# Later GpSimd clearings, a prepared double norm, a shorter output norm in the delta rule, and dilated attention's copies, scores and maxima re-ordered

## The reference

```python
# between the blocks: the last norm of the first, then the first norm of the second
x = rmsnorm(x, g_final)
h = rmsnorm_2(x, norm_mix[0])

# the end of the delta rule: 8 heads of 128, forward and backward sums
o = jnp.transpose(o_fwd + o_bwd, (0, 2, 1, 3))
o = o * lax.rsqrt(jnp.mean(o * o, axis=-1, keepdims=True) + RMS_EPS)
o = o * norm_w.astype(f32) * jax.nn.silu(z.astype(f32))
return o.reshape(B, S, H * DV).astype(h.dtype) @ w_out

# dilated attention: 3 groups of heads (dilation 1, 4, 16), 6 heads each
s = jnp.einsum('nbqhe,nbkhe->nbhqk', qb, kw).astype(jnp.float32) * (E ** -0.5)
s = s + bias[None, None]
m = jnp.max(s, axis=-1, keepdims=True)
lse = m + jnp.log(jnp.sum(jnp.exp(s - m), axis=-1, keepdims=True))
p = jnp.exp(s - lse)
o = jnp.einsum('nbhqk,nbkhe->nbqhe', p.astype(v.dtype), vw)
alpha = jax.nn.softmax(jnp.stack(lses, axis=2), axis=2)
```

## Time and profile before

| what | value |
|---|---|
| median of 3 runs | 1920.75 us (1918.34 to 1920.76) |
| the profiled execution | 1922.57 us, span from first to last instruction 1920.8 us |
| TensorE busy | 1862.0 us, 97% of the span |
| VectorE, ACT, GpSimd busy | 1312.5 us (68%), 907.3 us (47%), 22.6 us (1%) |
| mean granted TensorE clock | 0.984 of full |
| HBM | 161 GB/s over the span |

### The profile page before, as it was taken

The page is one execution under the profiler, slowest core; times in us unless marked ns, Lnnn a source line. Parts: engine busy times, 40 slices in busy tenths (PEclk is TensorE's granted clock), DMA queues, the critical chain, the costliest instruction groups (busy, mean ns, idle before and its releaser), DMA issues. The chain is left out here.

```text
span 1920.8 us, 30237 instructions
## 1 busy us (share of the span) xinstructions
PE 1862.0 (97%) x12455; PEld 1699.2 (88%) x12455; DVE 1312.5 (68%) x2105; ACT 907.3 (47%) x1233; POOL 22.6 (1%) x25
## 2 busy tenths in 40 slices
PE   7999999999999999999999989999899999999998
PEld 7999898999999999988888879878888889779887
DVE  5657874999788888755555567986577455647754
ACT  6457633342444343444444455766365343445533
POOL 0000000000000000000000000010000001000000
PEclk9999999999999999999999998997999999999999
DMA  6444344444444444465555552420254456615543
GB/s 231 176 157 157 132 176 177 153 179 173 154 154 141 148 153 154 154 229 197 191 188 191 194 202 91 152 88 24 73 190 175 177 214 201 146 69 205 187 164 152
DMA packets 44755, 310.63 MB, mean 162 GB/s; under 512 B 5182, under 2 KB 5694, under 8 KB 8160
## 3 DMA queue, kind: packets, MB, share of 16 engines
q1 hardware_dynamic: 42592, 303.58, 43.2%
q0 software_dynamic: 1472, 4.86, 1.6%
q10 hardware_dynamic: 576, 0.55, 0.1%
HBM read 306.84 MB, written 2.13 MB: 161 GB/s over the span
## 5 line engine op out<-in xcount | busy, mean ns | idle before, releaser
L310 DVE TENSOR_TENSOR s_ring_lo<-s_ring,s_w_hi 128x2048 fp32r<-128x2048 f32 x233 | 533.4, 2290 | 190.7 <-ACT s_w_hi L304 186.2
L304 ACT ACTIVATE s_w_hi<-s_ring 128x2048 fp32r<-128x2048 f32 x232 | 442.8, 1909 | 141.4 <-PE bank L347 46.2
L347 PE MATMUL bank<-s_h_r,s_w_hi 128*128 128x256 f32 x2944 | 391.0, 286 | 0.3 <-DVE s_arena L3454 0.3
L347 PEld LDWEIGHTS bank<-s_h_r,s_w_hi 128*128 128x128 f32 x2944 | 368.1, 193 | 4.8 <-issue 3.6
L1711 PE MATMUL bank<-s_w_hi,s_h_r 128*128 128x512 f32 x1008 | 238.8, 389 | 0.3 <-issue 0.3
L1711 PEld LDWEIGHTS bank<-s_w_hi,s_h_r 128*128 128x128 f32 x1008 | 189.2, 188 | 39.6 <-issue 0.4
L347 PE MATMUL bank<-s_h_r,s_ring_lo 128*128 128x256 f32 x1472 | 207.0, 283 | 0.0
L347 PEld LDWEIGHTS bank<-s_h_r,s_ring_lo 128*128 128x128 f32 x1472 | 190.4, 193 | 0.0
L1813 ACT ACTIVATE s_h_r<-s_arena 128x512 fp32r (+1 forms) x64 | 40.4, 632 | 184.5 <-PE bank L1711 184.5
L2969 DVE TENSOR_TENSOR s_ring_lo<-s_ring,s_spare_r 128x2048 fp32r<-128x2048 f32 x32 | 73.1, 2291 | 77.0 <-ACT s_spare_r L2955 77.0
L1711 PE MATMUL bank<-s_ring_lo,s_h_r 128*128 128x512 f32 x504 | 124.5, 389 | 0.0
(11 more groups left out here) (448 smaller groups left out, 2446.0 us busy)
## 6 DMA issues: line engine op xcount, KB each, us to landing
s_ring<-weights SPq DMA_DIRECT2D x282, 1024.0 KB, 4.8
s_arena<-bias_by_distance POOLq DMA_DIRECT2D x12, 384.0 KB, 7.3
s_arena<-mem SPq DMA_DIRECT2D x1, 1024.0 KB, 5.7
s_x<-x SPq DMA_DIRECT2D x1, 1024.0 KB, 13.4
x_away<-s_x SPq DMA_DIRECT2D x1, 1024.0 KB, 6.4
s_arena<-sub_keys SPq DMA_DIRECT2D x1, 1024.0 KB, 8.4
s_arena<-x_away SPq DMA_DIRECT2D x1, 1024.0 KB, 6.9
out<-s_x SPq DMA_DIRECT2D x2, 512.0 KB, 2.6
```

The costliest lines, as they stand in the source:

```text
L304: act.activation(k.w_hi[:, u % 2, :], k.ring[:, u % RING, :], ACT.Copy).then_inc(k.hi_ready, 1)
L310: dve.tensor_tensor(k.ring_lo[:, u % RING, :], k.ring[:, u % RING, :], plain(k.w_hi[:, u % 2, :]), ALU.subtract).then_inc(k.lo_ready, 1)
L347: last = pe.matmul(out[:, nb * S:(nb + 1) * S], w[:, c, nb * P:(nb + 1) * P], h[:, c, :], start=(n == 0 and c == 0), stop=(n == 2 and c == 7))
```

## The change

1. The second and third clearing of GpSimd wait for the first unit of the delta rule's projection.
2. The double norm's second factor is written as 1 / (mean of the weighed squares + EPS times (mean + EPS)), which is the same number; its parts are prepared before the last squares are there.
3. In the read-out TensorE adds the state's part itself, as a product with the identity that opens the bank. ACT squares straight out of the bank and takes the root of mean + EPS in one step; VectorE takes the reciprocal and scales the outputs out of the bank; the turn is a plain transpose.
4. In the dilated layer the third group of `turn(0)` goes behind unit 11 (and its copy on ACT behind the evacuation of unit 11), `highest(4)` ahead of `weights(3)` and `split_out(1)`, and the third group of `score(5)` behind the first two of `turn(4)`.

```diff
@@ DoubleSeam.factors
-        m, t, both = self.mean[:, 0:2], self.inner[:, 0:2], self.both
+        raw, m, e, both = self.inner[:, 0:2], self.mean[:, 0:2], self.product[:, 0:2], self.both
         dve.wait_ge(self.x_squared, 4)
-        own.up(dve.tensor_tensor(m, self.x_sums[:, 0:2], self.x_sums[:, 2:4], ALU.add))
+        own.up(dve.tensor_tensor(raw, self.x_sums[:, 0:2], self.x_sums[:, 2:4], ALU.add))
         own.settle(dve)
-        own.up(dve.tensor_scalar(m, m, 1.0 / D, EPS, ALU.mult, ALU.add))
+        own.up(dve.tensor_scalar(e, raw, EPS / D, EPS * EPS, ALU.mult, ALU.add))
+        own.up(dve.tensor_scalar(m, raw, 1.0 / D, EPS, ALU.mult, ALU.add))
         own.settle(dve)
+        dve.wait_ge(self.w_squared, 2)
+        own.up(dve.scalar_tensor_tensor(out=e, in0=self.w_sums[:, 0:2], scalar=1.0 / D, in1=e, op0=ALU.mult,
+                                        op1=ALU.add))
         own.up(dve.reciprocal(both[:, 0:2], m))
+        own.settle(dve)
         dve.wait_ge(self.w_squared, 4)
-        own.up(dve.tensor_tensor(t, self.w_sums[:, 0:2], self.w_sums[:, 2:4], ALU.add))
+        own.up(dve.scalar_tensor_tensor(out=e, in0=self.w_sums[:, 2:4], scalar=1.0 / D, in1=e, op0=ALU.mult,
+                                        op1=ALU.add))
         own.settle(dve)
-        own.up(dve.tensor_tensor(t, t, both[:, 0:2], ALU.mult))
-        own.settle(dve)
-        own.up(dve.tensor_scalar(t, t, 1.0 / D, EPS, ALU.mult, ALU.add))
-        own.settle(dve)
-        own.up(dve.reciprocal(self.product[:, 0:2], t))
-        own.settle(dve)
-        dve.tensor_tensor(both[:, 2:4], self.product[:, 0:2], both[:, 0:2], ALU.mult).then_inc(self.factor_ready, 1)
+        dve.reciprocal(both[:, 2:4], e).then_inc(self.factor_ready, 1)
@@ gdn_project, gpsimd
         pool.memset(plain(g.unset), 0.0).then_inc(zeros_set, 1)
+        pool.wait_ge(k.unit_done, U["gdn_qkv"] + 1)
         pool.memset(plain(inv_r), 0.0).then_inc(inv_clear, 1)
@@ gdn_solve, tensor: read_out(q)
             pe.wait_ge(qs_out, q + 1)
+            pe.matmul(ps[4 + q][:, :], k.ident, group(from_state, q), start=True, stop=False)
...
@@ turn(q)
-            pe.wait_ge(diag_ready, q + 1)
+            pe.wait_ge(o_scaled, q + 1)
             for c in range(4):
-                last = pe.matmul(ps[q][:, c * P:(c + 1) * P], o[:, 4 * q + c, :], diag[:, q % 2, c, :],
-                                 start=True, stop=True)
+                last = pe.transpose(ps[q][:, c * P:(c + 1) * P], o[:, 4 * q + c, :], k.ident)
@@ scalar
         for q in range(GROUPS):
-            act.wait_ge(o_out, q + 1)
+            act.wait_ge(o_mm, q + 1)
             for c in range(4):
-                act.activation(junk[:, c, :], o[:, 4 * q + c, :], ACT.Square,
+                act.activation(junk[:, c, :], ps[4 + q][:, c * P:(c + 1) * P], ACT.Square,
...
-            act.wait_ge(o_means, q + 1)
-            act.activation(o_root[:, 4 * q:4 * q + 4], o_inv[:, 4 * q:4 * q + 4], ACT.Sqrt).then_inc(o_roots, 1)
+            act.wait_ge(o_square, 4 * (q + 1))
+            act.activation(o_root[:, 4 * q:4 * q + 4], o_sum[:, 4 * q:4 * q + 4], ACT.Sqrt, scale=1.0 / P,
+                           bias=o_eps[:, 0:1]).then_inc(o_roots, 1)
@@ vector
+        dve.memset(o_eps[:, 0:1], EPS).then_inc(eps_set, 1)
...
-            dve.wait_ge(o_mm, q + 1)
-            dve.wait_ge(qs_out, q + 1)
-            dve.tensor_tensor(group(o, q), ps[4 + q][:, :], group(from_state, q), ALU.add).then_inc(o_out, 1)
-            dve.wait_ge(o_square, 4 * (q + 1))
-            own.up(dve.tensor_scalar(o_mean[:, at], o_sum[:, at], 1.0 / P, EPS, ALU.mult, ALU.add))
+            dve.wait_ge(o_roots, q + 1)
+            own.up(dve.reciprocal(o_inv[:, at], o_root[:, at]))
             own.settle(dve)
-            dve.reciprocal(o_inv[:, at], o_mean[:, at]).then_inc(o_means, 1)
+            for c in range(4):
+                last = dve.tensor_scalar(o[:, 4 * q + c, :], ps[4 + q][:, c * P:(c + 1) * P],
+                                         o_inv[:, 4 * q + c:4 * q + c + 1], None, ALU.mult)
...
+            last.then_inc(o_scaled, 1)
             if q >= 1:
                 gate(q - 1)
             if q >= 2:
                 split_out(q - 2)
...
@@ ds_layer, tensor
-        turn(0)
+        turn(0, (0, 1))
         unit(11)
+        turn(0, (2,))
         score(2)
...
-        score(5)
+        score(5, (0, 1))
         turn(4, (0, 1))
+        score(5, (2,))
         weigh(3)
@@ scalar
-        turned_out(0)
+        turned_out(0, (0, 1))
         evacuate(11)
+        turned_out(0, (2,))
         turned_out(1, (0, 1))
@@ vector
         split_lo(k, dve, O)
+        highest(4)
         weights(3)
         split_out(1)
-        highest(4)
         split_lo(k, dve, O + 1)
```

More of the change, by code:

```diff
@@ L2396, in gdn_solve @@
     lay = Layout(k, g.at_kdec + 2 * H * S)
-    o, junk, diag = lay.take(2 * H, P), lay.take(4, P), lay.take(2, 4, P)
+    o, junk = lay.take(2 * H, P), lay.take(4, P)
     gated, from_state = carve(k, g.at_kdec, H, S), carve(k, g.at_kdec, 2 * H, P)
     oT = [k.spare_r[:, n * H * S:(n + 1) * H * S].rearrange("p (h s) -> p h s", h=H) for n in range(2)]
-    o_sum, o_mean, o_inv, o_root = (k.small[:, n * 16:(n + 1) * 16] for n in range(4))
+    o_sum, o_eps, o_inv, o_root = (k.small[:, n * 16:(n + 1) * 16] for n in range(4))
     names = ("decay_mm", "decays_ready", "keys_mm", "system_built", "third_turned", "solved_set",
@@ L2408, in gdn_solve @@
      wide_mm, wide_out, last_mm, level_done, v1_mm, v1_out, state_mm, state_out, ks_mm, rhs_ready, v2_mm, v2_out,
-     o_mm, o_out, o_square, o_means, o_roots, diag_ready, o_turned, o_gated, o_round, o_split,
+     o_mm, eps_set, o_square, o_roots, o_scaled, o_turned, o_gated, o_round, o_split,
      qs_mm, qs_out) = (ctx_sem(k, "g_" + n) for n in names)
@@ L2603, in read_out @@
                     pe.matmul(ps[4 + q][:, at], g.intraT[:, h, first_s[f], :], v1[:, 2 * h + f, :],
-                              start=True, stop=False)
+                              start=False, stop=False)
                     last = pe.matmul(ps[4 + q][:, at], g.intraT[:, h, second_s[s], :], v2[:, 2 * h + s, :],
-                                     start=False, stop=True)
+                                     start=False, stop=(hh == 1 and tt == TT - 1))
             last.then_inc(o_mm, 1)
         def turn(q):
-            pe.wait_ge(diag_ready, q + 1)
+            pe.wait_ge(o_scaled, q + 1)
             for c in range(4):
-                last = pe.matmul(ps[q][:, c * P:(c + 1) * P], o[:, 4 * q + c, :], diag[:, q % 2, c, :],
-                                 start=True, stop=True)
+                last = pe.transpose(ps[q][:, c * P:(c + 1) * P], o[:, 4 * q + c, :], k.ident)
             last.then_inc(o_turned, 1)
@@ L2633, in tensor @@
                 turn(q - 1)
-        pe.wait_ge(o_out, 2)
         pe.wait_ge(o_round, 2)
@@ L2638, in tensor @@
         turn(3)
-        pe.wait_ge(o_out, 4)
         pe.wait_ge(o_round, 4)
@@ L2750, in scalar @@
             act.activation(group(state, q), ps[4 + q][:, :], ACT.Copy).then_inc(state_out, 1)
+        act.wait_ge(eps_set, 1)
         act.activation(o_root[:, 0:1], k.ident[:, 0:1], ACT.Sqrt)
@@ L2886, in vector @@
             at = slice(4 * q, 4 * q + 4)
-            dve.wait_ge(o_mm, q + 1)
-            dve.wait_ge(qs_out, q + 1)
-            dve.tensor_tensor(group(o, q), ps[4 + q][:, :], group(from_state, q), ALU.add).then_inc(o_out, 1)
-            dve.wait_ge(o_square, 4 * (q + 1))
-            own.up(dve.tensor_scalar(o_mean[:, at], o_sum[:, at], 1.0 / P, EPS, ALU.mult, ALU.add))
-            own.settle(dve)
-            dve.reciprocal(o_inv[:, at], o_mean[:, at]).then_inc(o_means, 1)
+            dve.wait_ge(o_roots, q + 1)
+            own.up(dve.reciprocal(o_inv[:, at], o_root[:, at]))
+            own.settle(dve)
+            for c in range(4):
+                last = dve.tensor_scalar(o[:, 4 * q + c, :], ps[4 + q][:, c * P:(c + 1) * P],
+                                         o_inv[:, 4 * q + c:4 * q + c + 1], None, ALU.mult)
+                if c < 3:
+                    own.up(last)
+            last.then_inc(o_scaled, 1)
             if q >= 1:
@@ L2897, in vector @@
                 split_out(q - 2)
-            dve.wait_ge(o_out, q + 1)
-            dve.wait_ge(o_roots, q + 1)
-            for c in range(4):
-                last = dve.tensor_scalar(diag[:, q % 2, c, :], k.ident, o_root[:, 4 * q + c:4 * q + c + 1], None,
-                                         ALU.mult)
-                if c < 3:
-                    own.up(last)
-            last.then_inc(diag_ready, 1)
         gate(GROUPS - 1)
@@ L3191, in unit, with score @@
                 unit_N_split(k, pe, F + n, (k.hT_hi, k.hT_lo), [bank[:, 0:S], bank[:, S:2 * S]])
-        def score(j):
+        def score(j, groups=range(G)):
             rows = out_rows(j)
-            for g in range(G):
+            for g in groups:
                 q = G * j + g
```

2 lines of the change are left out of this document (1 added, 1 removed).

## The result

The changed kernel takes **1903.4 us** (median of 5 runs, 1903.26 to 1905.88), the kernel before, beside it, 1918.68 us (1913.79 to 1920.76, 5 runs): ratio 0.9917, 95% interval 0.9905 to 0.993. The forecast was 1908.0 with a range from 1904.5 to 1912.5. The profiled execution took 1904.64 us around a span of 1902.0, so the two profiled executions lie 17.9 us apart and the two medians 15.3.

What follows compares the result with a forecast made beforehand. TensorE is busy nearly throughout, so only waits in front of it count. 1.9 + 2.1 + (2.3 + 2.0 + 0.8) + 4.6 = 13.7 us off 1922.57 gives 1908.9, lowered to 1908 for the profiled run's excess; range 1904.5 to 1912.5.

Steps and rivals of the forecast that it cites:

- 1.3 + 0.6: Double norm: root starts earlier, some 1.3 us from the moved clearing and 0.6 from the shorter chain, 1.9 together.
- The hold: Projection's third unit: VectorE's tensor_scalar held by the moved clearings ends 1.2 us late; 1.4 us of cover remain, cost 0.
- The bound of 1.6 us for held splits: Projection: if VectorE's tensor_tensor splits beside the clearings were held too, the sum would lose at most 1.6 us.
- a forecast of 2.1: Delta rule's read-out: the output product's second half starts 2.1 us earlier through the shorter output norm.
- The loop: Read-out, per group: squares, root, reciprocal, scalings, gate, rounding and hand-overs through ACT and VectorE take 4.15 us.
- the identity product took over 1 us: Read-out: sign that the forecast is wrong; TensorE's 128x512 f32 product with the identity was counted at 0.88 us.
- (a): Dilated layer: with unit 11 put between, TensorE's 2.35 us wait for ACT's copies at the third turn goes; gain 2.3.
- (b): Dilated layer: with highest(4) moved ahead, TensorE's 2.00 us wait for VectorE before the third score goes; gain 2.0.
- (c): Dilated layer: score(5)'s third group behind turn(4) leaves waits of 0.4 and 0.65 in place of 1.82 us; gain 0.8.
- The rival that the clock falls all the same: Dilated layer: low clock returns despite the new order; one stretch costs 1.7 to 2.9, both 4.6: 1910 to 1912.5 us; 24%.
- term (d): Dilated layer: two stretches at 1.2 GHz go with the waits of 2.00 and 1.82 us; gain 4.6 (2.9 + 1.7).
- a low stretch elsewhere: Double norm or read-out: a shorter stretch at low clock, as their waits shrink, could take the time down to 1904.5 us.

Runs made afterwards that it cites:

- delayed by 6 steps: Changed kernel with six extra small VectorE steps ahead of the double norm's factors: 1910.16 us, ratio 0.9941.
- the spread kernels: Gates' 2 x 24 products issued in four runs of 12: on the changed kernel 1906.02 us, with six extra VectorE steps 1905.66, with the read-out's gate first 1901.65.
- maxima alone: Kernel before with only highest(4) moved ahead of weights(3) and split_out(1): 1919.73 us, ratio 0.9992.
- norm alone: Kernel before with only the delta rule's shorter output norm (identity product, scalings out of the bank): 1918.56 us, ratio 1.0003.
- dilated alone: Kernel before with only the dilated layer's new order: 1911.54 us, ratio 0.9959.

## Why the prediction came out as it did

**Double norm, clearings.** Right in both parts: 1.35 + 0.53 us measured for 1.3 + 0.6, and the clearings cost nothing at their new place. The hold is as foreseen: a tensor_scalar beside the memset 1.13 us in place of 0.17, a tensor_tensor of 0.42 us not held. This agrees with the Trainium skill ("SBUF — State Buffer", section "Who interferes with whom"). The bound of 1.6 us for held splits had no cause. The prediction took the hold's whole length as lateness (1.2 us); the step ended 0.96 us later than it would have (1.13 - 0.17).

**Output norm.** 2.42 us between the two profiles, for a forecast of 2.1; 0.7 of them is the low clock in the last turn before, so the chain itself gave 1.8, and the agreement is partly luck. The loop came out at 4.06 us for 4.15 because prices that were off cancel. From start to start the squares take 1.16 (1.3 taken), the root 0.33 (0.25), the scalings 1.04 (1.0; their row shows the upper bound, 1.12), the gate 0.78 (0.7), the rounding 0.54 (0.6). The prediction called itself wrong if the identity product took over 1 us. Its row shows 1.02, but that counts its end as well; the next product starts 0.86 us behind it, and 0.88 was taken. The PSUM operand costs as the Trainium skill has it ("VectorE: DVE Perf Modes", section "Why PSUM operands drop a tier"): 1.12 us from the bank, 0.87 from SBUF.

**Dilated layer.** By the start of the same work in both traces: (a) 2.56 us for 2.3, (b) and the slow score behind it 2.92, (c) 1.11, the clock behind unit 13 and in the last weighing 1.74 + 1.40. The sum is 9.7 us, and 2.3 + 2.0 + 0.8 + 4.6 was 9.7. The division differs: part of the 4.6 lies in the score that stood behind the wait (2.07 us for four products, 1.13 in the changed kernel). The rival that the clock falls all the same did not come, in none of nine profiled kernels with this order; with two of the three waits left it does. The 4.6 was the price of one execution's low stretches (10.2 us long); with the same layer another execution had 3.4.

**What failed: the sum took the low clock in the dilated layer alone.** The prediction's term (d) priced low clock only there, and the sum has no term for the other low stretches. The places that it costed give 1.9 + 2.4 + 9.7 = 14.0 us; 13.7 was forecast. The spans differ by 18.8. The rest is clock elsewhere:

- Behind the gates: 1.63 + 1.36 = 3.0 us. The prediction had the row of 3.23 us in hand, used it as the time at which TensorE wants the unit, and did not ask why sixteen products took 3.23 us there. All four profiled kernels with the clearings at their old place have a loss there, and of the seven with the later clearings and runs of 24 six have none (the seventh is the one delayed by 6 steps). So the traces show that the loss goes with the timing of the double norm; that the run of short products is what makes the clock fall is likely (see the spread kernels), and what sets the moment is open.
- Behind the double norm: 0.64 us. The x16 of L556 took 3.78 us and takes 2.79. My range spoke of it ("a low stretch elsewhere") and gave it too little.
- Ahead of everything changed: GpSimd's first clearing starts at 1145.89 in place of 1147.34. 1.45 us is no effect of the change. Windows of the kernel before and of the one after, at the same work:

```profile
303.50:307.00 3.50, 3.50 (x10) 2.79 (x9) 0.92 (x5) 1.42 (x2) 0.00 (x0) 0.51 1.00 398
```

```profile
293.00:313.00 20.00, 17.89 (x112) 16.25 (x111) 2.36 (x7) 6.98 (x21) 0.00 (x0) 1.00 0.66 239
```

That makes 5.1 us; 14.0 + 5.1 = 19.1, 0.3 above the 18.8. With the 0.7 in the last turn, 5.8 us of it are clock outside the dilated layer.

**The base.** I took half of the 1.8 us between the profiled execution and the median off, since a part of it was clock that I already counted. In the comparison the kernel before came to 1918.68 us, not the 1921.7 that I started from: 3.0 us of the 4.6 between 1908.0 and 1903.4. The gain between the medians is 15.3 us for 13.7: the other 1.6. Over all its 58 runs the kernel before has a median of 1919.55; by that the base is 2.2 of the miss and the gain 2.4. So the medians show less of the 5.1 us of clock than the two traces do; how much of the gates' 3.0 us an average run of the kernel before pays is open: of the profiled executions with the old clearings and double norm, two had low stretches behind both runs of short products (the kernel before, maxima alone) and two behind the first only (norm alone, dilated alone).

## What to carry to other kernels

A group of equal matmuls that takes half again its usual time is a row to explain, not a time to read off: list such rows over the whole span, and treat what stands ahead of each (a wait, or a run of short products) as worth the wait plus some of the low clock behind it. Remove all such waits of a layer together, since those that are left can keep much of the loss. And when a change moves a stage by a microsecond, give the stages behind it that sit near the edge a term of both signs. Spreading short products among large ones may make a stage less sensitive to where it lands; here it did no harm to the stage. And before a difference of medians is given a cause, compare the mean clocks of the runs.

## What the hardware showed that I had not expected

- The clock falls without any wait of TensorE: 24 products of 128x32, back to back in 2.75 to 3.22 us, are followed by 3.2 and 6.1 us at 0.50 (1.2 GHz) in one kernel (L2181, the delay of 6 steps) and by none in another that runs the same stage at another time (the changed kernel, 2.75 and 2.85 us).
- With a delay of 1.4 us the median rose by 6.8 us (5.1 of stage time in the trace on top of the wait), with one of 2.5 us by 4.7.
- In every kernel the runs of one program spread by some us (before: 1915.96 to 1924.03 over 28 runs), as much as parts of this change are worth; the traces resolve steps of 0.5 us that the medians do not. The spread goes with the clock: over the 53 runs of the kernel before beside the experiments the fastest (1915.96 to 1916.15) have a mean granted clock of 0.988, the slowest (1923.87 to 1924.12) 0.983 or 0.984.
